# Two lower halves per recurrent layer made by VectorE instead of GpSimd, in a two-block transformer kernel

## The reference

```python
proj = h @ w_in[l]
c_q, c_kv, k_pe, hq, hf, hi, hg = jnp.split(proj, splits, axis=-1)
...
z = f_raw.astype(F32)
lb = lower_bound.astype(F32)
f = lb + (1.0 - lb) * jax.nn.sigmoid(z)
log_f = jnp.log(jnp.maximum(f, F_FLOOR))
k = (1.0 - lb) * jax.nn.sigmoid(-z)
...
b = jnp.cumsum(lfb, axis=2)
...
o = _rmsnorm(o, out_norm) * jax.nn.silu(g_raw.astype(F32).reshape(B, S, HG_HEADS, HG_VAL))
```

## Time and profile before

| | us |
|---|---|
| median of three runs | 1930.76 |
| lowest and highest run | 1929.14, 1933.79 |
| the profiled execution, its time | 1933.04 |
| its span on the core | 1931.1 |
| VectorE's lower halves by line 1809, 135 of them, busy | 163.8 |
| GpSimd's lower halves by line 632, 134 of them, busy | 343.0 |

### The profile page before, as it was taken

The page is one execution under the profiler, slowest core; times in us unless marked ns, Lnnn a source line. Parts: engine busy times, 40 slices in busy tenths (PEclk is TensorE's granted clock), DMA queues, the critical chain, the costliest instruction groups (busy, mean ns, idle before and its releaser), DMA issues.

```text
span 1931.1 us, 27217 instructions
## 1 busy us (share of the span) xinstructions
PE 1892.8 (98%) x9931; PEld 1610.5 (83%) x9931; DVE 1501.8 (78%) x1598; ACT 1244.5 (64%) x1473; POOL 392.2 (20%) x204
## 2 busy tenths in 40 slices
PE   8999999999999999999899999999999999999997
PEld 6788889998888999878788888888888888888885
DVE  7755366666765756697599999999999999899997
ACT  5654444445644444564388887888888888888885
POOL 5856870002823000372430000000000000000000
PEclk9999999999999999999899999999999999999999
DMA  9434556664443766434399999999999999999994
GB/s 279 154 130 131 175 185 214 216 225 153 140 125 122 226 214 215 156 119 141 131 377 394 382 395 357 395 396 355 395 354 396 396 353 395 355 395 395 358 395 175
DMA packets 251402, 524.54 MB, mean 272 GB/s; under 512 B 10009, under 2 KB 58785, under 8 KB 251185
## 3 DMA queue, kind: packets, MB, share of 16 engines
q1 hardware_dynamic: 244000, 506.36, 73.5%
q10 hardware_dynamic: 5088, 10.03, 1.4%
q0 software_dynamic: 2224, 6.96, 1.1%
HBM read 508.12 MB, written 15.20 MB: 271 GB/s over the span
## 4 chain that ended last, share of the span: by engine, by line
PE 90%; DVE 6%; issue 2%; ACT 2%; POOL 1%; DMA 0%; DVEq 0%; SPq 0%; ACTq 0%
PE bank L696 27%; PE bank L698 27%; PE bank L697 27%; PE bank L1049 2%; PE bank L1222 1%; DVE w_lo_sb L1797 1%; PE bank L770 1%; PE bank L743 1%; PE bank L749 1%; POOL w_lo_sb L632 1%; ACT w_hi_sb L1359 0%; PE bank L1102 0%; PE bank L1100 0%; PE bank L904 0%; PE bank L881 0%
## 5 line engine op out<-in xcount | busy, mean ns | idle before, releaser
L1797 DVE TENSOR_TENSOR w_lo_sb<-arena,w_hi_sb 128x1024 fp32r<-128x1024 f32 x672 | 806.8, 1223 | 73.8 <-ACT w_hi_sb L1359 47.6
L1359 ACT ACTIVATE w_hi_sb<-arena 128x1024 fp32r<-128x1024 f32 x672 | 710.5, 1062 | 165.1 <-PE bank L698 164.6
L696 PE MATMUL bank<-w_hi_sb,left_hi_sb 128*128 128x512 f32 (+1 forms) x1424 | 563.9, 396 | 7.5 <-POOL w_lo_sb L632 3.0
L698 PE MATMUL bank<-w_hi_sb,left_lo_sb 128*128 128x512 f32 (+1 forms) x1424 | 552.7, 388 | 0.0
L697 PE MATMUL bank<-w_lo_sb,left_hi_sb 128*128 128x512 f32 (+1 forms) x1424 | 552.1, 388 | 0.0
L1379 ACT ACTIVATE w_hi_sb<-arena 128x1024 fp32r<-128x1024 f32 (+1 forms) x269 | 280.3, 1052 | 336.6 <-PE bank L698 325.2
L632 POOL TENSOR_TENSOR w_lo_sb<-arena,w_hi_sb 128x1024 fp32r<-128x1024 f32 (+1 forms) x134 | 343.0, 2580 | 566.2 <-ACT w_hi_sb L1379 565.7
L696 PEld LDWEIGHTS bank<-w_hi_sb,left_hi_sb 128*128 128x128 f32 x1424 | 268.4, 188 | 66.4 <-issue 6.3
L698 PEld LDWEIGHTS bank<-w_hi_sb,left_lo_sb 128*128 128x128 f32 x1424 | 268.2, 188 | 56.1
L697 PEld LDWEIGHTS bank<-w_lo_sb,left_hi_sb 128*128 128x128 f32 x1424 | 268.5, 189 | 52.2 <-issue 0.7
L1809 DVE TENSOR_TENSOR w_lo_sb<-arena,w_hi_sb 128x1024 fp32r<-128x1024 f32 x135 | 163.8, 1219 | 126.1 <-ACT w_hi_sb L1379 125.1
(11 more groups left out here) (328 smaller groups left out, 1628.3 us busy)
## 6 DMA issues: line engine op xcount, KB each, us to landing
arena<-in_moe_w_gate SPq DMA_DIRECT2D x112, 1024.0 KB, 7.8
arena<-in_moe_w_up SPq DMA_DIRECT2D x112, 1024.0 KB, 7.8
arena<-in_moe_w_down SPq DMA_DIRECT2D x112, 1024.0 KB, 7.6
arena<-in_w_in SPq DMA_DIRECT2D x45, 1024.0 KB, 5.1
arena<-in_w_ffn_in SPq DMA_DIRECT2D x22, 1024.0 KB, 6.2
arena<-in_w_out SPq DMA_DIRECT2D x12, 1024.0 KB, 5.0
arena<-in_w_ffn_out SPq DMA_DIRECT2D x11, 1024.0 KB, 4.8
arena<-in_dense_w_gate SPq DMA_DIRECT2D x11, 1024.0 KB, 5.9
```

The costliest lines, as they stand in the source:

```text
L696: pe.matmul(out, still[0], moving[0], start=start, stop=False)
L698: return pe.matmul(out, still[1], moving[0], start=False, stop=stop)
L1359: act.activation(expert_buffer(w_hi_sb, j), expert_piece(j % MOE_SUBS), ACT.Copy) \
L1797: dve.tensor_tensor(expert_buffer(w_lo_sb, j), expert_piece(j % MOE_SUBS), expert_buffer(w_hi_sb, j).bitcast(F32), ALU.subtract) \
```

## The change

In each of the two layers the first two pieces of the gate product (hg) get their lower halves from VectorE. The condition that picks the maker is widened, and three calls of `lo_to` place the work in VectorE's chain: the first piece after the absolute value in both layers, the second after `n_lf` in layer 0 and after the product with `bound_rest` in layer 1. GpSimd's loop skips these four pieces, TensorE waits for them on the other counter, and so does SyncE for the one load in each layer whose slot they free.

```diff
     for j, (_, _, piece) in enumerate(subs):
-        by_vector = j < FIRST_SUBS or any(lo + BUFFERS <= j < hi + AFTER_FFN for lo, hi in ffn_range.values())
+        by_vector = j < FIRST_SUBS or any(lo + BUFFERS <= j < hi + AFTER_FFN for lo, hi in ffn_range.values()) \
+            or any(0 <= j - span[f"hg_{l}"][0] < 2 for l in range(2))
...
                 absolute(tiles(n_tmp[0]), n_z, "z_abs")
                 soft = tiles(n_tmp[1])
+                lo_to(span[f"hg_{l}"][0] + 1)
                 if l == 0:
                     dve.wait_ge(sem("z_soft"), 1)
                     dve.scalar_tensor_tensor(n_lf, n_z, 0.0, soft, ALU.min, ALU.subtract).then_inc(sem("n_lf_ready_0"), 1)
+                    lo_to(span["hg_0"][0] + 2)
                     dve.scalar_tensor_tensor(n_k, n_z, 0.0, soft, ALU.max, ALU.add).then_inc(sem("n_k_ready"), 1)
...
                     mul(share, share, over(bound_rest, 1, T))
+                    lo_to(span["hg_1"][0] + 2)
                     dve.wait_ge(sem("z_soft"), 2)
```

## The result

| | before | after |
|---|---|---|
| median of 16 runs each on the same chip, us | 1929.69 | 1934.66 |
| lowest and highest run, us | 1929.11, 1933.79 | 1932.31, 1936.46 |
| the profiled execution, its span, us | 1931.1 | 1930.3 |
| ratio after to before, 95% interval | | 1.0022 [1.0015, 1.0029] |

The change makes the kernel slower by 0.22%, some 4 to 5 us. The profiled execution of the changed kernel took 1932.31 us, the fastest of its 16 runs, so the two spans alone would say "faster". The traces must be compared stretch by stretch.

The account below looks back on a forecast made before the run. TensorE, busy 98% of the span, bounds the kernel, so only its stops count. Layer 0 +3.8 and layer 1 -2.0 give +1.8 us on the median 1930.76: 1932.6 us, range 1928.0 to 1936.5.

Parts of the forecast that it names:

- Layer 0's chain: VectorE's chain to the copy of the first sum in layer 0: copy at 505.22 instead of 501.44, 3.8 us later.
- The replay in strict turns: Layer 0: VectorE (1.12 us) and GpSimd (2.37 us) take whole instructions in turn at a shared port; gives the copy at 505.22.
- TensorE's idle of "some 5 us": Layer 0, ahead of the fifth bank's product: TensorE would stand some 5 us in place of 1.4.
- the second piece is the dear one: Layer 0: VectorE's second new piece stands in front of line 2131, where VectorE had no wait to fill.
- Layer 1: TensorE's sums in layer 1: six VectorE instructions run without a wait as GpSimd has nothing to do; 2.0 us earlier.
- The rival that trading work between these engines does not help there: Layer 1 gains nothing and only layer 0's loss stays: +3.8, 1934.6 us; chance 0.05.
- What cost nothing: SyncE's wait on the other count, ScalarE's order, TensorE's changed counter and the removed GpSimd time: no effect on time.
- the late fourth query piece: Layer 0: GpSimd's piece ends at 489.40 instead of 488.28; TensorE loses about 0.6 us, hidden in the later stop.
- the clock: Rival: granted clock falls to half rate in layer 0's new stop, costing 1 to 4 us; +2.8 to +5.8, 1934.6 us; chance 0.30.
- The two rivals that named 1934.6 us: Clock falling in layer 0's stop (chance 0.30) and no gain in layer 1 (0.05), each +3.8 us.
- The argument against: Against a falling clock in layer 0's stop: over 945 to 950 us TensorE was busy only 3.47 us, still at full clock.
- slower by over 0.2%: Whole kernel: chance 0.20 of a measured loss over 0.2%; within 0.73, faster 0.07.

Follow-up runs that it names:

- layer 1 alone: The change with layer 0's two pieces left to GpSimd, so only layer 1's go to VectorE, against the kernel before: 1929.52 us, ratio 0.9995.
- layer 1 with the cure: Kernel before with only layer 1's two pieces given to VectorE and the bounds' softmax sum and reciprocal moved ahead of the logarithm wait: 1926.93 us, ratio 0.9984.
- layer 0 alone: Only layer 0's two gate pieces go to VectorE, layer 1's stay with GpSimd, against the kernel before: 1934.90 us, ratio 1.0023.
- delay of 256 columns: Kernel before plus an unused 256-column reciprocal (1.7 us) in VectorE's chain ahead of the first sum's copy, no piece moved: 1932.80 us, ratio 1.0013.
- delay of 512: Kernel before plus an unused 512-column reciprocal (3.35 us) in VectorE's chain ahead of the first sum's copy, no piece moved: 1936.31 us, ratio 1.0030.
- both layers with the cure: The whole change plus the bounds' softmax sum and reciprocal moved ahead of the logarithm wait, against the kernel before: 1929.53 us, ratio 0.9997.
- the cure alone: Kernel before with the bounds' softmax sum and reciprocal moved ahead of VectorE's wait for the logarithm, no piece moved: 1928.54 us, ratio 0.9991.

## Why the prediction was right, and where it was short

- **Layer 0's chain.** Forecast +3.8 us at the copy, measured +3.3. The replay in strict turns holds event by event. With 3.29 us added for the earlier start, the first new piece ends at 487.03 (forecast 487.03), `n_lf` at 490.38 (490.52), the second piece at 493.76 (494.01), `n_k` at 497.10 (497.50), the reciprocal at 503.27 (503.82) and the copy starts at 504.75 (505.22). The 0.5 us too much is the sum of some 0.1 us per turn. TensorE's idle of "some 5 us" was 5.03. That the second piece is the dear one held too: it costs 2.4 of the 3.3 us, the first 0.9.
- **Layer 1.** Forecast -2.0, measured -1.9, twice more in layer 1 alone and in layer 1 with the cure. The four VectorE lines took 1.2 us. The rival that trading work between these engines does not help there is out. The warning of the Trainium skill (Perfetto Trace Analysis, Optimizing Scalar/DVE Operations) holds in layer 0 and not in layer 1; what differs is whether GpSimd has its next piece ready.
- **What cost nothing** did cost nothing: the late fourth query piece was hidden in the stop.
- **The step that fell short** is the clock. The prediction kept it as a rival with 0.30 and left it out of the sum, as a term of 0. It fell in the profiled execution of the changed kernel and in all three others with a stop of 3.2 us or more at that place. It cost 1.4 to 2.9 us in them, inside the rival's bounds of 1 to 4. With it the sum would have been 3.3 - 1.9 + 1.4 to 2.9 = +2.8 to +4.3 us; the measured ratio gives +4.2 [+2.9, +5.6]. So the range held the time, but the likeliest number, +1.8, was too low, and slower by over 0.2% deserved more than 0.20. Part of the nearness of 1932.6 to 1934.66 us is luck: the sum started from a median of three runs, 1930.76, which 16 runs put at 1929.69, so the forecast missed the time by 2.1 us and the change by 2.4 to 3.2. The two rivals that named 1934.6 us cannot be told apart by the time; the traces do it, since layer 1 gained its 1.9 us and the clock was low. The argument against, that the clock was full over 945 to 950 us with 3.47 us busy, spoke of a stretch in which TensorE worked for the most part; in the new one it had stood still for 4.6 us when the clock fell. The rule of the Trainium skill, TensorE: Matmul & The Clock Gate, HAM oscillation, gave the better forecast here: the trace agrees with it (a stop of 5.03 us, and 1.2 GHz until 505.2 us).

**Open.** How often the clock falls at this stop could not be counted, as one execution of each kernel has a trace and the others only a mean. Nor is it shown where the runs of layer 1 alone give back all of their 1.2 us: its trace shows some 0.5 us of it between 950 and 965 us, and the fall near 586 us, which came in two other kernels' executions, is a candidate for the rest. What decides whether and when the clock falls in a stop is not shown either.

## What to carry to other kernels

Work traded from GpSimd to VectorE pays where GpSimd then has nothing queued (-1.9 us in layer 1). Where its next pieces are ready it costs VectorE's chain the work of each piece (0.9 us for the one put into a wait) and a turn of GpSimd as well for the one put where VectorE did not wait, +3.3 us in all in layer 0, whatever idle time VectorE shows ahead. Before filling a wait with more work, look in the same chain for work that nobody waits for yet and move that into the wait: the moved softmax gained 2.2 us with no piece moved. And price a new stop of TensorE with the clock behind it, not by its length alone: in the four kernels with a stop of 3.2 to 5.0 us at this place it added 1.4 to 2.9 us in the profiled execution, up to 2.9 us on a delay of 3.4.

## What the hardware showed unexpectedly

- A stop of 3.24 us between dense products came with 1.2 GHz for 6.8 us (the delay of 256 columns), and one of 5.03 us with only half of that (the changed kernel): its length alone does not set the price. Stops of 1.43, 2.66 and 2.77 us in this stretch kept 2.4 GHz.
- The clock fell 2.3 us (delay of 256), 2.6 (layer 0 alone), 4.2 (delay of 512) and 4.6 us (the changed kernel) into the stop, and the price is half of what is left of the low clock once TensorE works again: 2.9, 2.3, 3.1 and 1.5 us by that reckoning, 2.8, 2.2, 2.9 and 1.4 measured.
- The clock after layer 0's attention (near 586 us) fell in the executions of layer 1 with the cure and of both layers with the cure. It did not fall in that of the cure alone, whose matmuls there are those of layer 1 with the cure, 0.09 us apart. So an execution can lose 1.6 us at a place that the edit does not touch.
- The turns of VectorE and GpSimd are regular enough to be replayed over seven instructions to within 0.5 us, with 1.12 and 2.37 us for a piece.
